# Recurrent mixer's projections: order of the mixtures, key norms by head, and the tail before the scan

## The chip, the cores and the metric

One core of a Trainium2 chip runs the whole program. The metric is the device time of one execution in microseconds; the time of a kernel is the median of its runs. One further execution was taken with the profiler on, and all durations of single instructions are from that one.

## The reference

The program computes two transformer blocks one after the other on 256 tokens of 1024 features. The change touches one part of the second block, the projections in front of an RWKV-7 scan, over 256 context tokens and 256 latent tokens (512 columns):

```python
def rwkv_project(h, shifted, mu, w_rkv, w0, w1, w2, a0, a1, a2, g1, g2, kvec):
    xx = shifted - h
    xr, xw, xk, xv, xa, xg = (h + xx * mu[i] for i in range(6))
    r = xr @ w_rkv[0]
    k = xk @ w_rkv[1]
    v = xv @ w_rkv[2]
    lw = jnp.einsum("zblr,zrd->zbld", jnp.tanh(jnp.einsum("bld,zdr->zblr", xw, w1)), w2) + w0[:, None, None, :]
    decay = jnp.exp(-jnp.exp(-jax.nn.softplus(-lw.astype(jnp.float32)) - 0.5))
    a = jax.nn.sigmoid(a0 + (xa @ a1) @ a2)
    g = jax.nn.sigmoid(xg @ g1) @ g2
    kk = to_heads(k * kvec[0], RW_HEADS).astype(jnp.float32)
    kk = kk / jnp.maximum(jnp.sqrt(jnp.sum(kk * kk, axis=-1, keepdims=True)), 1e-12)
    k = k * (1 + (a - 1) * kvec[1])
```

There are 16 heads of 64 features. The output needs for each head also the bonus, the sum over the head of r k kvec[2], times v, on the latent tokens only; so r and g are computed for 256 columns and k, v, a and the decays for 512.

## The kernel before

The program is written per engine: five instruction streams (TensorE, ScalarE, VectorE, GpSimd and the SyncE queue that issues the loads), each in an order written out by hand, joined by semaphores. `Line` (L63) makes each VectorE, ScalarE and GpSimd instruction wait for the one before it on the same engine. `Tensor.bank` (L159) makes TensorE wait, before it writes one of the eight PSUM banks, for whoever reads the last contents. `mm` is the matrix product (L165 in the profile), `tr` the transpose, here called a turn (L170). VectorE's operations have one line each: `tt` L87 (a product, sum or difference of two tensors), `tsc` L92 or L94, `stt` L98, `copy` L102, `recip` L115. ScalarE's are L138 and L144.

Weights come through a ring of five slots of 128x2048 fp32 (1 MB), in the order that `tile_plan` (L191) lists. SyncE takes the list in turn: it waits until the slot's last tile is used up (`w_free`), then issues the load. `HELD_OUT` (L253) pins the slots of the last tiles, because the scan's scratch lies in slots 0 to 2.

The part around the change is `rwkv_pe` (L2698), `rwkv_act` (L2786) and `rwkv_dve` (L2832). The features lie on the 128 partitions, in 8 tiles, the 512 tokens along the row. One "feature" is one such tile of an output: 8 products of 128x128 weights by 512 columns into one bank (`features`, L2774). The order in which the parts come:

1. VectorE makes the differences XX and then the mixtures h + xx mu, eight `stt` each (`mix`, L2825), in the order of `MIXES` (L2306): w (1), g (5, latent half), a (4), k (2). Two buffers, XMAT[0] and XMAT[1], take them in turn.
2. TensorE does the low-rank products in the order w, g, a (`LOW`, L2307), ScalarE reads them with Tanh, Sigmoid and Copy, and TensorE makes a from the copy (ra2: eight products whose contraction is 64 rows). ScalarE reads each with Sigmoid.
3. TensorE does the eight key features into banks 0 to 3. For each, ScalarE writes KK = key times kvec[0], and VectorE makes K from a and the bank, and the square of KK.
4. The norm block. Eight products with `bones` (ones in two 64x64 blocks) spread each head's sum of squares over its 64 partitions, ScalarE takes eight roots of 128x512, and VectorE does for each tile a maximum, a reciprocal (128x512), and the products into KK and AK. Then VectorE makes the mixtures r (0, latent half) and v (3).
5. TensorE does the eight receptance features (256 columns), then the eight value features (512). Even tiles are copied out by ScalarE, odd ones by VectorE.
6. After the values: VectorE makes r k kvec[2] for 8 tiles, TensorE sums them by head (`bones`), VectorE multiplies with the values; then TensorE turns the values in eight groups of four 128x128 blocks, and VectorE copies each out in four pieces of 64x256.
7. `decay_pe(T, 0)` (L2383): 16 products of 512 columns whose contraction is 64 rows, two into each bank; ScalarE reads each bank with Sigmoid (`decay_act`, L2397). `decay_pe(T, 1)`, the same for the other direction, is issued inside the scan.
8. The scan (`scan_pe`, L2403, and its fellows), two groups of heads against each other through `lead` (L2690), in 17 rounds.

The order of steps 4 and 5 in VectorE's stream is what the change takes apart:

```python
            for k in range(8):
                x = XM[0][:, k, :]
                ve.wait_ge(*n3_ok[k])
                D.tsc(x, x, 1e-12, None, ALU.max, None)
                D.recip(x, x)
                D.tt(KK[:, k, :], KK[:, k, :], x, ALU.mult)
                D.tt(AK[:, k, :], AK[:, k, :], KK[:, k, :], ALU.mult, n4_ok(k))
            mix(D, 4, 256)
            mix(D, 5)
```

In this `mix` the number is a place in `MIXES`, so 4 and 5 are the receptance's and the values' mixtures. `mod_pe` (L933) is not touched; the prediction uses a row of it: a modulation tile is four products of 512 columns over 128 rows into four groups of 32 output rows, set between features of the feed-forward layers.

## Time and profile before

| | |
|---|---|
| median of 3 runs | 3262.8 us (3256.42, 3262.8, 3263.97) |
| the profiled execution | 3254.83 us, its span 3253.0 us |
| TensorE products busy | 2911.7 us, 90% |
| TensorE weight loads busy | 2441.5 us, 75% |
| VectorE busy | 1697.1 us, 52% |
| ScalarE busy | 1215.8 us, 37% |
| GpSimd busy | 117.7 us, 4% |
| mean granted TensorE clock | 0.94 |
| DMA | 349.86 MB, mean 108 GB/s |
| 1 MB weight tile of rkvr, issue to landing | 4.8 us |

The part of the change lies between about 2178 and 2460 us of the span, the scan after it up to about 2955. Busy shares are averages over the whole span. A product of 512 columns in fp32 is recorded as two records, so a feature of 512 columns is 16 records. The end of a product's record is modelled and reaches past the start of the next; the step from start to start is its cost in a full stream. The clock column of a window is the granted share of 2.4 GHz: 1.00 is that level, 0.50 is 1.2 GHz.

### The profile page before, as it was taken

The numbers are of one execution on the slowest core, as the hardware profiler recorded it, in microseconds if no ns is written. First come the engines' busy times: TensorE is split into PE (matmuls) and PEld (weight loads), VectorE is DVE, ScalarE is ACT, GpSimd is POOL, SyncE is SP. The second block draws the span as 40 slices with busy tenths as digits, with TensorE's granted clock in tenths as the row PEclk, the third lists the DMA queues.
The fourth block names the chain that finished last, engine by engine and source line by source line (L and its number), as shares of the span: only waits on it lengthen the run. The fifth ranks groups of instructions, "written<-read, shape, count | busy, mean of one in ns | idle before, by whom it ended". The sixth has DMA issues, their size and how long they took to land.

```text
span 3253.0 us, 65485 instructions
## 1 busy us (share of the span) xinstructions
PE 2911.7 (90%) x28272; PEld 2441.5 (75%) x28272; DVE 1697.1 (52%) x2488; ACT 1215.8 (37%) x1831; POOL 117.7 (4%) x152
## 2 busy tenths in 40 slices
PE   6999999999999989988878998959489999997898
PEld 6977799898778977766657776844337998994886
DVE  4545555454655544215647775443623554555885
ACT  4445554444564443324433323331003334331333
POOL 0000000000000000000000000000001221220000
PEclk9999999999999999989889999979787999998999
DMA  5544344455443543430012432202100000002342
GB/s 208 183 168 170 130 166 178 171 185 187 149 156 137 182 156 133 177 105 2 10 52 91 155 143 108 86 25 102 39 26 9 4 4 16 4 4 95 128 154 104
DMA packets 49983, 349.86 MB, mean 108 GB/s; under 512 B 5792, under 2 KB 5792, under 8 KB 9248
## 3 DMA queue, kind: packets, MB, share of 16 engines
q1 hardware_dynamic: 49248, 343.56, 29.6%
q8 instruction: 225, 3.69, 0.5%
q0 software_dynamic: 448, 2.10, 0.2%
q14 instruction: 62, 0.51, 0.0%
HBM read 344.59 MB, written 1.05 MB: 106 GB/s over the span
## 4 chain that ended last, share of the span: by engine, by line
PE 78%; DVE 13%; ACT 5%; issue 2%; DMA 1%; DVEq 0%; SPq 0%; ACTq 0%
PE psum L165 77%; DVE wide L87 2%; DVE arena L98 2%; DVE arena L87 2%; DVE ring_low L87 2%; ACT w_high L144 1%; DVE wide L115 1%; DMA ring<-in_evt 1%; DVE wide L102 1%; ACT wide L138 1%; ACT arena L140 1%; DVE wide L98 1%; PE psum L170 1%; DMA ring<-in_f_gu 1%; ACT wide L144 0%
## 5 line engine op out<-in xcount | busy, mean ns | idle before, releaser
L87 DVE TENSOR_TENSOR ring_low<-ring,w_high 128x2048 fp32r<-128x2048 f32 (+3 forms) x254 | 560.3, 2206 | 595.9 <-ACT w_high L144 591.3
L144 ACT ACTIVATE w_high<-ring 128x2048 fp32r<-128x2048 f32 (+3 forms) x254 | 468.9, 1846 | 834.3 <-PE psum L165 485.7
L165 PE MATMUL psum<-x_high,w_high 128*128 128x256 f32 (+1 forms) x2040 | 634.3, 311 | 13.4 <-DVE arena L87 6.7
L165 PE MATMUL psum<-x_high,ring_low 128*128 128x256 f32 (+1 forms) x2040 | 627.1, 307 | 0.0
L165 PE MATMUL psum<-x_low,w_high 128*128 128x256 f32 (+1 forms) x2040 | 627.0, 307 | 0.0
L165 PE MATMUL psum<-wide,ring 64*64 64x64 f32 (+2 forms) x4400 | 414.8, 267 | 77.2 <-DVE wide L98 43.1
L165 PEld LDWEIGHTS psum<-x_high,w_high 128*128 128x128 f32 x2040 | 390.7, 192 | 49.9 <-issue 16.8
L165 PEld LDWEIGHTS psum<-wide,ring 64*64 64x64 f32 (+1 forms) x4400 | 296.0, 146 | 172.1 <-issue 97.1
L165 PEld LDWEIGHTS psum<-x_high,ring_low 128*128 128x128 f32 x2040 | 390.6, 191 | 18.6
L165 PEld LDWEIGHTS psum<-x_low,w_high 128*128 128x128 f32 x2040 | 390.9, 192 | 17.2
L165 PE MATMUL psum<-w_high,x_high 128*128 128x512 f32 (+2 forms) x720 | 281.3, 391 | 15.7 <-issue 13.8
L165 PE MATMUL psum<-ring_low,x_high 128*128 128x512 f32 (+2 forms) x720 | 276.9, 385 | 0.0
L165 PE MATMUL psum<-w_high,x_low 128*128 128x512 f32 (+2 forms) x720 | 276.9, 385 | 0.0
L165 PE MATMUL psum<-wide 64*64 64x64 f32 (+3 forms) x6832 | 242.2, 219 | 9.6 <-ACT wide L144 4.7
L165 PEld LDWEIGHTS psum<-wide 64*64 64x64 f32 (+2 forms) x6832 | 215.0, 133 | 25.5 <-ACT wide L144 8.9
L98 DVE SCALAR_TENSOR_TENSOR arena<-arena,prm 128x256 f32<-128x256 f32 x396 | 192.1, 485 | 14.1
L144 ACT ACTIVATE wide<-psum 128x256 f32<-128x256 f32 (+2 forms) x239 | 108.5, 454 | 225.2 <-PE psum L165 216.6
L165 PEld LDWEIGHTS psum<-w_high,x_high 128*128 128x128 f32 x720 | 139.9, 194 | 52.9 <-issue 23.3
L165 PE MATMUL psum<-w_high,h_high 128*128 128x512 f32 x440 | 172.5, 392 | 4.3 <-DVE ring_low L87 4.3
L165 PE MATMUL psum<-w_high,h_low 128*128 128x512 f32 x440 | 171.9, 391 | 0.0
L165 PE MATMUL psum<-ring_low,h_high 128*128 128x512 f32 x440 | 171.9, 391 | 0.0
L87 DVE TENSOR_TENSOR wide<-wide,psum 128x256 f32<-128x256 f32 (+1 forms) x156 | 86.0, 551 | 159.5 <-PE psum L165 153.7
(191 smaller groups left out, 3498.2 us busy)
## 6 DMA issues: line engine op xcount, KB each, us to landing
ring<-in_f_gu SPq DMA_DIRECT2D x88, 1024.0 KB, 4.8
ring<-in_w_mod SPq DMA_DIRECT2D x48, 1024.0 KB, 5.0
ring<-in_fu SPq DMA_DIRECT2D x44, 1024.0 KB, 4.8
ring<-in_f_dn SPq DMA_DIRECT2D x40, 1024.0 KB, 4.8
ring<-in_w_in SPq DMA_DIRECT2D x28, 1024.0 KB, 4.8
ring<-in_fd SPq DMA_DIRECT2D x20, 1024.0 KB, 4.8
ring<-in_rkvr SPq DMA_DIRECT2D x12, 1024.0 KB, 4.8
ring<-in_w_out SPq DMA_DIRECT2D x8, 1024.0 KB, 4.8
```

Source lines behind the costliest of these rows:

```text
L87: self.done(self.eng.tensor_tensor(o, a, b, op), then)
L98: self.done(self.eng.scalar_tensor_tensor(out=o, in0=a, scalar=s, in1=b, op0=op0, op1=op1), then)
L102: self.done(self.eng.tensor_copy(o, i), then)
L115: self.done(self.eng.reciprocal(o, i), then)
L138: self.done(self.eng.activation(o, i, f, bias=bias, scale=scale), then)
L140: self.done(self.eng.activation(o, i, f, bias=bias, scale=scale, accum_out=total), then)
L144: self.done(self.eng.activation(o, i, ACT.Copy, scale=scale), then)
L165: ins = self.eng.matmul(o, l, r, start=a, stop=z)
L170: ins = self.eng.transpose(o, i, ident[0:i.shape[0], 0:i.shape[0]])
```

## The change

The projections are put in another order and three pieces are done otherwise.

- Mixtures come in the order a, k, w, g, r, v. The products of w and g stand between key features (after the second and the fourth); the tiles rw1 and rg1 move in the load order behind the first and second key tile.
- Key norms: ScalarE squares each key tile out of the bank beside writing KK (six buffers SQUARES). One product per tile with `hs`, 128 rows by 16 columns, adds its heads' sums into one 16x512 block of bank 6, behind the feature two later. One root, one maximum and one reciprocal are taken on 16 rows. Products with a column of the identity, spread over 64 columns, and the 16-row block as moving operand spread each head's value over its 64 partitions, two products per tile, behind receptance features 4 to 7.
- The values' buffer VT moves from XX to another place. After the values, eight rounds on TensorE hold one decay bank, one group of turns and one bonus sum. ScalarE reads the decays and copies one half of the turned values, VectorE the other half and makes the bonus product.
- Two dummy activations on one column (Sqrt, Sigmoid) stand ahead of those uses. The signals are named anew.

The diff, cut (renamed signals, the unchanged halves of moved helpers and assertions of room are left out):

```diff
-    plan.append((("rw1",), dr["rw1"], 1024))
-    plan.append((("rg1",), dr["rg1"], 1024))
     plan.append((("ra1",), dr["ra1"], 512))
     plan.append((("ra2",), dr["ra2"], 1024))
     for i in (1, 0, 2):
-        plan.extend((("rkv", i, j), dr["rkvr"][i, j], WS) for j in range(4))
+        for j in range(4):
+            plan.append((("rkv", i, j), dr["rkvr"][i, j], WS))
+            if i == 1 and j < 2:
+                name = ("rw1", "rg1")[j]
+                plan.append(((name,), dr[name], 1024))
...
-        VT = XX
+        VT = wide[:, 25856:29952].rearrange("p (k t) -> p k t", k=8)
+        SQUARES = [wide[:, 29952 + 512 * i:30464 + 512 * i] for i in range(6)]
+        ROOTS = wide[0:16, 25344:25856]
...
+        MIXES = (4, 2, 1, 5, 0, 3)
+        LOW = {4: ("ra1", 64, 0), 1: ("rw1", 128, 4), 5: ("rg1", 128, 5)}
+        BESIDE_KEYS = {1: 1, 3: 5}
...
+        def head_sums(T, k):
+            if k == 0:
+                T.eng.wait_ge(ld_cxb, 16)
+                T.bank(6, rw_act["root", 0])
+            T.eng.wait_ge(*rw_act["kk", k])
+            T.mm(bank(6)[0:16, :], hs[:, 14 - 2 * k:30 - 2 * k], SQUARES[k % 6], k == 0, k == 7, rw_mm(("kk", k)))
...
         def rwkv_pe(T):
+            low_rank(T, 4)
...
             te.wait_ge(*mix_ok[2])
-            features(T, 1, XM[1], 0, kp_mm, k_ok, None)
-            te.wait_ge(ld_cxb, 16)
             for k in range(8):
-                te.wait_ge(*n1_ok[k])
-                T.bank(4 + k % 4, n3_ok[k])
-                T.mm(bank(4 + k % 4), bones, XM[0][:, k, :], True, True, n2_mm(k))
+                feature(T, 1, k, XM[1], 512, k_ok[k])
+                if k > 1:
+                    head_sums(T, k - 2)
+                if k in BESIDE_KEYS:
+                    low_rank(T, BESIDE_KEYS[k])
+            for k in (6, 7):
+                head_sums(T, k)
             te.wait_ge(*mix_ok[0])
-            features(T, 0, XM[0], 256, rp_mm, r_d, r_a)
+            for k in range(8):
+                feature(T, 0, k, XMH[1], 256, rw_dve["r", k] if k % 2 else rw_act["r", k])
+                if k == 4:
+                    te.wait_ge(*rq_ok[0])
+                for j in (2 * k - 8, 2 * k - 7) if k > 3 else ():
+                    T.bank(4 + j % 4, n4_ok[j])
+                    for a in TWO:
+                        T.mm(bank(4 + j % 4)[64 * a:64 * a + 64, :], ident[0:16, 2 * j + a:2 * j + a + 1].to_broadcast([16, 64]),
+                             ROOTS, True, True, rw_mm(("kb", j)) if a else None)
             te.wait_ge(*mix_ok[3])
-            features(T, 2, XM[1], 0, vp_mm, v_d, v_a)
             for k in range(8):
-                te.wait_ge(*bv1_ok[k])
-                T.bank(4 + k % 4, bv_ok[k])
-                T.mm(bank(4 + k % 4)[:, 0:256], bones, BV[:, k, :], True, True, bv_mm(k))
...
-            te.wait_ge(*vz_ok[3, 1])
-            decay_pe(T, 0)
+                feature(T, 2, k, XM[1], 512, rw_dve["v", k] if k % 2 else rw_act["v", k])
+            te.wait_ge(*rw_act["v", 6])
+            te.wait_ge(*rw_dve["v", 7])
+            for i, (tb, g) in enumerate(ITEMS):
+                decay_item_pe(T, 0, tb, g, 4 + i % 4)
+                T.bank(i % 2, rw_dve["vz", i], vz_a[i])
+                trs(T, [(bank(i % 2)[:, 128 * a:128 * a + 128], VT[:, 4 * g + a, 128 * tb:128 * tb + 128]) for a in FOUR],
+                    rw_mm(("vz", i)))
+                T.bank(2 + i % 2, rw_dve["bv", i])
+                te.wait_ge(*rw_dve["rk", i])
+                T.mm(bank(2 + i % 2)[:, 0:256], bones, BV[:, i, :], True, True, rw_mm(("bv", i)))
+            te.wait_ge(*rw_dve["bv", 7])
+            te.wait_ge(*vz_a[7])
             lead(scan_pe(T, 0), scan_pe(T, 1))
...
         def rwkv_act(A):
             for k in range(8):
                 se.wait_ge(*tile_done(1, k))
-                A.act(KK[:, k, :], bank(k % 4), ACT.Identity, kk_ok(k), scale=kv[:, 0, k:k + 1])
-            for k in range(8):
-                se.wait_ge(*n2_mm[k])
-                A.act(XM[0][:, k, :], bank(4 + k % 4), ACT.Sqrt, n3_ok(k))
+                A.act(KK[:, k, :], bank(k % 4), ACT.Identity, scale=kv[:, 0, k:k + 1])
+                if k > 5:
+                    se.wait_ge(*rw_mm["kk", k - 6])
+                A.act(SQUARES[k % 6], bank(k % 4), ACT.Square, rw_act(("kk", k)), scale=kv[:, 0, k:k + 1])
+                if k in BESIDE_KEYS:
+                    low_act(A, BESIDE_KEYS[k])
+            A.act(small[:, 216:217], ident[:, 0:1], ACT.Sqrt)
+            se.wait_ge(*rw_mm["kk", 7])
+            A.act(ROOTS, bank(6)[0:16, :], ACT.Sqrt, rw_act(("root", 0)))
...
+            A.act(small[:, 216:217], ident[:, 0:1], ACT.Sigmoid)
+            for i, (tb, g) in enumerate(ITEMS):
+                decay_item_act(A, 0, tb, g, 4 + i % 4)
+                se.wait_ge(*rw_mm["vz", i])
+                value_rows(A, i, 0, vz_a(i))
...
         def rwkv_dve(D):
+            mix(D, 4, XM[0])
+            mix(D, 2, XM[1])
+            ve.wait_ge(*w_free[("ra1",)])
+            mix(D, 1, XM[0])
             for k in range(8):
...
-                if k == 0:
-                    ve.wait_ge(*w_free[("ra1",)])
-                D.tt(XM[0][:, k, :], KK[:, k, :], KK[:, k, :], ALU.mult, n1_ok(k))
+                if k == 1:
+                    ve.wait_ge(*w_free[("rw1",)])
+                    mix(D, 5, XMH[0], 256)
+                if k == 3:
+                    mix(D, 0, XMH[1], 256)
+            ve.wait_ge(*rw_act["root", 0])
+            D.tsc(ROOTS, ROOTS, 1e-12, None, ALU.max, None)
+            D.recip(ROOTS, ROOTS, rq_ok(0))
+            ve.wait_ge(*w_free["rkv", 1, 3])
+            mix(D, 3, XM[1])
+            for k in (1, 3):
+                receptance_block(D, k)
+            for j in (0, 1):
+                unit_keys(D, j)
+            receptance_block(D, 5)
+            for j in (2, 3, 4, 5):
+                unit_keys(D, j)
+            receptance_block(D, 7)
+            for j in (6, 7):
+                unit_keys(D, j)
...
+            for i in range(8):
+                ve.wait_ge(*rw_mm["vz", i])
+                value_rows(D, i, 1, rw_dve(("vz", i)))
+                if i == 0:
+                    ve.wait_ge(*rw_act["v", 6])
+                ve.wait_ge(*rw_mm["bv", i])
+                D.tt(BV[:, i, :], bank(2 + i % 2)[:, 0:256], VT[:, i, 256:512], ALU.mult, rw_dve(("bv", i)))
```

`unit_keys` waits for its spread root and does the two products into KK and AK; `receptance_block` waits for a receptance feature and copies it out; `value_rows` copies two 64x256 pieces of the turned values. In the new `mix` the number is the mixture's own.

## Rows read from the trace of the kernel before

**Rows 1.** The page's part 4: the chain that ended last, by engine.

```profile
PE 78%; DVE 13%; ACT 5%; issue 2%; DMA 1%; DVEq 0%; SPq 0%; ACTq 0%
```

**Rows 2.** Windows: stretch, length, busy time of each engine (instructions), granted clock, DMA.

```profile
2183.79:2216.48 32.69, 29.01 (x64) 12.46 (x64) 16.02 (x25) 7.66 (x11) 0.00 (x0) 0.86 0.28 97
2216.48:2271.72 55.24, 55.24 (x130) 24.62 (x130) 13.47 (x21) 5.50 (x8) 0.00 (x0) 1.00 0.22 76
2271.72:2321.64 49.92, 6.83 (x16) 2.66 (x14) 47.13 (x44) 6.75 (x10) 0.00 (x0) 0.60 0.06 21
2321.64:2351.75 30.11, 30.11 (x129) 26.16 (x130) 7.27 (x11) 1.53 (x4) 0.00 (x0) 0.93 0.31 105
2351.75:2406.69 54.94, 54.90 (x128) 23.94 (x126) 2.50 (x5) 3.67 (x5) 0.00 (x0) 1.00 0.05 20
2406.69:2431.10 24.41, 9.80 (x49) 6.46 (x49) 21.49 (x49) 0.00 (x0) 0.00 (x0) 0.81 0.13 43
2431.10:2459.45 28.35, 27.66 (x32) 10.36 (x32) 0.00 (x0) 4.78 (x8) 0.00 (x0) 0.50 0.00 0
2459.45:2472.50 13.05, 8.60 (x126) 7.67 (x128) 3.23 (x6) 3.63 (x6) 1.77 (x2) 0.50 0.12 41
...
2209.45:2216.48 7.03, 7.03 (x16) 2.88 (x16) 0.00 (x0) 4.81 (x7) 0.00 (x0) 1.00 0.44 151
```

**Rows 3.** Groups of instructions by form, VectorE, 2160 to 2460: busy us, mean ns, idle before.

```profile
L115 DVE RECIPROCAL wide<-wide 128x512 f32<-128x512 f32 x8 | 26.8, 3353 | 0.3
L98 DVE SCALAR_TENSOR_TENSOR wide<-wide,prm 128x512 f32<-128x512 f32 x32 | 24.1, 752 | 7.0 <-PE psum L165 5.9
L87 DVE TENSOR_TENSOR wide<-wide 128x512 f32<-128x512 f32 x24 | 16.6, 692 | 0.9
L102 DVE COPY wide<-psum 64x256 f32<-64x256 f32 x32 | 13.5, 422 | 1.6
...
L87 DVE TENSOR_TENSOR wide<-psum,wide 128x256 f32<-128x256 f32 x8 | 3.4, 425 | 0.9
```

**Rows 4.** Timeline, ScalarE: start, length, form, idle before and releaser.

```profile
2193.80 0.60 ACT L138 ACTIVATE wide<-psum 128x512 f32<-128x512 f32 x1 [23.27 <-PE psum L165]
```

**Rows 5.** The chain in order of time: start, length, what.

```profile
2208.72 0.73 issue
```

**Rows 6.** Timeline, TensorE, around one modulation tile.

```profile
1752.69 0.39 PE L165 MATMUL psum<-x_low,w_high 128*128 128x512 f32 x1
1752.92 0.39 PE L165 MATMUL psum<-x_high,ring_low 128*128 128x512 f32 x1
1753.23 1.07 PE L165 MATMUL psum<-ring,arena 128*32 128x512 f32 x8
1754.23 0.50 PE L165 MATMUL psum<-x_high,w_high 128*128 128x512 f32 x1
1754.57 0.39 PE L165 MATMUL psum<-x_low,w_high 128*128 128x512 f32 x1
```

**Rows 7.** Groups by form, ScalarE, 2160 to 2460.

```profile
L138 ACT ACTIVATE wide<-psum,prm 128x512 f32<-128x512 f32 x16 | 11.0, 687 | 52.1 <-PE psum L165 52.1
...
L138 ACT ACT_TABLE_LOAD x5 | 6.4, 1283 | 0.4
```

**Rows 8.** Timeline, TensorE, turns of the values.

```profile
2414.41 1.91 PE L170 MATMUL psum<-cst,wide 128*128 128x128 f32 x16
```

**Rows 9.** Windows again: second decays; after the values; around a modulation tile.

```profile
2685.50:2699.50 14.00, 14.00 (x36) 5.90 (x32) 0.42 (x1) 4.89 (x8) 0.00 (x0) 1.00 0.00 0
...
2420.00:2431.00 11.00, 2.60 (x12) 1.56 (x10) 9.87 (x24) 0.00 (x0) 0.00 (x0) 0.58 0.00 0
1740.00:1780.00 40.00, 40.00 (x190) 30.46 (x189) 28.08 (x48) 11.85 (x14) 0.00 (x0) 1.00 0.40 144
```

**Rows 10.** Timeline, TensorE, groups of 32 records in the scan.

```profile
2466.62 1.97 PE L165 MATMUL psum<-wide 64*64 64x64 f32 x32 [0.79 <-DVE wide L87]
...
2681.44 1.10 PE L165 MATMUL psum<-wide 64*64 64x64 f32 x32
```

More of the change, by code:

```diff
@@ L2695, in tile_done, with low_rank, feature @@
         def tile_done(i, k):
-            return w_free["rkv", i, k // 2] if k % 2 else {1: kp_mm, 0: rp_mm, 2: vp_mm}[i][k // 2]
+            return w_free["rkv", i, k // 2] if k % 2 else rw_mm["rkv"[i], k]
+        def low_rank(T, i):
+            name, rows, b = LOW[i]
+            te = T.eng
+            te.wait_ge(*landed((name,)))
+            te.wait_ge(*mix_ok[i])
+            w = raw((name,))
+            x, cols = (XMH[0], 256) if i == 5 else (XM[0], 512)
+            T.bank(b, rw_act["low", i])
+            for k in range(8):
+                T.mm(bank(b)[0:rows, 0:cols], w[:, rows * k:rows * k + rows], x[:, k, :], k == 0, k == 7,
+                     w_free((name,)) if k == 7 else None)
+        def feature(T, i, k, x, cols, taken):
+            key = ("rkv", i, k // 2)
+            T.eng.wait_ge(*landed(key))
+            w = raw(key)
+            T.bank(k % 4, taken)
+            for c in range(8):
+                o = 256 * c + 128 * (k % 2)
+                T.mm(bank(k % 4)[:, 0:cols], w[:, o:o + 128], x[:, c, :], c == 0, c == 7,
+                     None if c < 7 else w_free(key) if k % 2 else rw_mm(("rkv"[i], k)))
+        def head_sums(T, k):
[4 more added lines that the diff above has]
+            T.mm(bank(6)[0:16, :], hs[:, 14 - 2 * k:30 - 2 * k], SQUARES[k % 6], k == 0, k == 7, rw_mm(("kk", k)))
         def rwkv_pe(T):
@@ L2887, in rwkv_dve @@
[L2887 to L2897 removed]
+                D.copy(VT[:, k, :], bank(k % 4), rw_dve(("v", k)))
```

168 lines of the change are left out of this document (70 added, 98 removed).

## The prediction

> **What bounds the kernel now.** I read the chain that ended last first: 78% of the span is TensorE, 13% VectorE [rows 1]. As an average that says nothing of the edited stage, so I cut that stage out by windows of the span [rows 2]. TensorE is full (busy time equal to the window) in four of the eight stretches: key features 55.24, receptance 30.11, values 54.94, decays about 28. It is not full in the other four: 32.69 us from the first mixture to the first key feature, 49.92 us between the last key feature and the first receptance feature, 24.41 us after the values, and the step into the scan. In the 49.92 and the 24.41 VectorE is busy 47.13 and 21.49 us: it is the bound there. Of its rows in the region [rows 3], 8 reciprocals of 128x512 take 26.8 us, 3.35 each. The decay stretch is full but runs at clock 0.50, the 1.2 GHz level, after a stretch in which TensorE was mostly waiting.
>
> **The change part by part.** Durations are those of the profiled execution (3254.83 us, span 3253.0), 8 us under the 3262.8 median, inside the spread of the three runs (7.5 us) but for half a microsecond. The change's sum is made on it and taken off the median.
>
> *A, mixtures by need.* Before, keys start 32.69 us after the first mixture. Now VectorE makes mixture 4 first (about 6.3 us as before, 0.2 later for the small okv operation) and TensorE runs ra1 at once: 8 products of 512 columns out of a cold start. The first low-rank group before took 10.0 us from 2183.79 to its reader at 2193.80 [rows 4]. Then the copy of TA, 0.73 us of TensorE's time [rows 5], then the eight ra2 products, 7.03 us (2209.45 to 2216.48, the last of [rows 2]). Keys start after 0.2 + 10.0 + 0.73 + 7.03 = 18.0 us. Mixture 2 (6.3 us) is long made, mixture 1 ends about 16.5 us in. **-14.7 us.** The DMA queue: the two moved loads stand behind k0 and k1 in it, the first five slots still fill in the feed-forward tail, rg1 waits only for ra1's slot and k2 for ra2's; both are free 20 us or more before use, and a load of 1 MB lands in about 5 us (4.8, table ahead). I cost the queue at nothing. If a slot came late the keys would wait for that one load, 5 us.
>
> *B, the key stage gets longer.* rw1 and rg1 move in: 8 products at 55.24/64 = 0.86 us, and 8 at half the columns, 6.9 + 3.4 = 10.3 us. Eight head sums move in: 0.86 each for 512 columns, however few the output rows. They change the array's shape in the middle of full features. A row that shows such a change is the modulation tile [rows 6]: four products in four column groups, eight records, start at 1753.23; the feature before started at 1752.92 and the second after at 1754.57, and of these 1.65 us two steps of 0.23 (1752.69 to 1752.92) were due anyway, so tile and changes took 1.19 us against 0.86 for one product: up to 0.34 for in and out. The step into and out of ra2 shows 0.17 (7.03 against 8 x 0.86). I take 0.25. The Trainium skill, "TensorEngine Tiling (Array Packing)", section "Key Properties", says that changing the tiling mode drains TensorE, and it speaks against this change; the trace agrees, at these prices. The round trips number 8 here, 4 in the receptance stage and 8 in the tail: 5.0 us in all, ends 0 and 6.8. Stage B: 10.3 + 8 x 1.11 = **+19.2 us**. ScalarE has two 512-wide passes per feature, 0.69 us each [rows 7], and up to three table loads of 1.28; its turn is 6.9 us, so nothing waits. VectorE's mixtures 5 and 0 (half the columns, so under the 6.3 us of a whole one) fit between two key tiles likewise. The last head sum needs the square of tile 7, 1.4 us after the last feature, and two sums stand before it: no wait.
>
> *C, the norm block.* The 49.92 us goes: receptance features need only mixture 0, made beside the keys. What becomes of its VectorE work: 8 squares (0.69, as every 512-wide product [rows 3]) move to ScalarE; 8 reciprocals become one on 16 rows, same 512 columns, so about 3.4 us; 16 products of 128x512 stay (11 us), and mixture 3 (6.3 us) with them. They now stand beside receptance, 35 us long. The chain root, maximum, reciprocal ends 5 us into it and mixture 3 at 11; TensorE asks for the first spread root at 17. Eight pairs of products at 1.4 us follow pairs of spreads, each behind a 3.4 us feature. What would be late next is the value stage's first bank, and it is not. **-49.9 us.**
>
> *D, receptance.* Eight features of half width from a warm start: 8 x 3.43 = 27.5. Eight spread roots come in, each of two products of 512 columns on the same 16 rows into two column halves. No row has 16 rows by 64 columns. Ends: side by side 0.86 for the two, one after the other 1.72. The nearest row is the modulation tile, four products over the same 128 rows in four column groups in little more than one product's time [rows 6], so I take 0.86: 8 x 0.86 + 4 x 0.25 = 7.9. 35.4 against 30.1: **+5.3 us**, serial +12.2.
>
> *E, values.* 54.94 us stay.
>
> *F, the tail.* Before: 52.8 us from the last feature to the scan, 24.41 and 28.35. Bonus sums, 32 turn copies of 0.42 and eight bonus products stood on VectorE in a row with TensorE waiting, then 16 decay products at 1.2 GHz. Now eight rounds of two decay products, four turns and one bonus sum. Warm, 1.72 + 0.48 (four turns; 16 took 1.91 [rows 8]) + 0.43 + 0.25 = 2.9 us. ScalarE has three passes of at most 0.69 in a round [rows 7], VectorE two copies of 0.42 and a product of 0.43: both under 2.9, so TensorE sets the pace. 0.75 for the last value's copy, 8 x 2.88 = 23.0, and 0.9 for the last copies and product: 24.7. **-28.1 us.** The eight products r k kvec (under 0.75 each, the whole-width row of their kind [rows 3]) move under the values, covered by 55 us.
>
> Warm is the assumption. A decay's product on 64 rows ran at 1.2 GHz before, all 28 us, and did not rise. But the same 16 products for the other direction, issued inside the scan with the clock up, ran 14.0 us at 1.00 [rows 9]. And the stage before this tail is the value stage, at 1.00. So I take warm; cold costs 8 x 2.63 = 21 us more.
>
> *G, start of the scan.* The first scan round ran at the low level to 2472.5 [rows 2]: 32 records took 1.97 us there, 1.10 later [rows 10]. About five such groups stood on the chain, so up to 4 us come back if the clock is still up. The round waits much, and the clock fell in the waiting stretch 2420 to 2431 [rows 9]. Ends 0 and 4; I take 3. **-3 us.**
>
> Sum: -14.7 + 19.2 - 49.9 + 5.3 - 28.1 - 3.0 = **-71.2 us**, a span near 3182, and 3262.8 - 71.2 = 3191.6.
>
> **The rivals.**
>
> *1. Spread roots one after another.* The two halves share their rows. For it: no row has this shape. Against it: [rows 6]. It costs 8 x 0.86 = 6.9 us: 3198.5. The Trainium skill, "TensorE: Matmul & The Clock Gate", section "Part 3: Packing small matmuls — row/col tiling", says a weight load overlaps running products only when its row group differs, which would make this the case; the modulation tile, same rows and four column groups, speaks against the rule. Chance 0.13.
>
> *2. The tail runs at 1.2 GHz.* The decays before did so while full. The 0.75 us wait, or the 64-row products with turns between, would let the clock fall. Cost 21 us, and the 3 of G: 71.2 - 24 = 47.2, 3215.6. Against it: ra2's 64-row products and the second decays stayed at 1.00 [rows 2, 9]. Chance 0.10.
>
> *3. Slower.* The clock falls in the key stage, where 16-column sums cut the features, and stays down. Then every feature costs double: keys with what moved in +74, receptance +35, values +55, in all 164 us, of which the 71 gained are only a part: about 3355. It decides from the point where 81 us of warm work (the 71 and 10 more) run at the low level, that is all of the keys and a quarter of receptance. For it: the 28 full microseconds at 0.50. Against it: the window 1740 to 1780 with a modulation tile between features is at 1.00 [rows 9], and the key features ran at 1.00 right after 64-row products [rows 2]. Chance 0.03: 0.02 for that much or more, 0.01 for a fall that eats between 61 and 81 us and leaves the time within 0.3%.
>
> *4. The 49.9 us is not freed,* because receptance waits for something in the norm chain after all: a spread root's bank, or mixture 3 ahead of VectorE's copies of banks 1 and 3. The order written out leaves VectorE some 4 us at the tightest place: its copy of bank 3 ends 14.2 us into the stage, the first spread root 18.2. If half came back as waits, 46 us would be left, 3217; if all, 21, 3241. Chance 0.04.
>
> **How the numbers follow.** The forecast's case has 0.70. The low end of the range is that case with no cost for shape changes (5 us) and the whole 4 us of G, 3185.6, and the 6.4 us by which the fastest run lies under the median: 3179. The high end takes in rivals 1 and 2: 3216. Left out are rivals 3 and 4 and the far sides. This kernel's measurement tells a difference from about 0.3%, 10 us. Faster by more than that: 0.96 (the forecast's case, rivals 1 and 2, and 0.03 of rival 4); within: 0.02 (0.01 of rival 3, and 0.01 of rival 4 for waits beyond those I can name); slower: 0.02.
>
> **What would show it.** Right: no gap of over 3 us between the last key feature and the first receptance feature; one reciprocal of 16x512 near 3.4 us in place of eight; first key feature near 2202; scan's first product near 2391; decay records at 1.02 us length, clock 1.00 from 2194 on. Spread roots: starts of two pairs 0.9 us apart, or 1.7 for rival 1. Wrong: decay records at the low level (rival 2); clock under 1.00 in the features (rival 3); TensorE's idle time in receptance ended by VectorE's products or reciprocal (rival 4).

## The result and the profile after

| | before | after |
|---|---|---|
| median of 4 runs each | 3262.32 us (3256.42 to 3263.97) | 3188.69 us (3182.56 to 3193.04) |
| the profiled execution | 3254.83 us, span 3253.0 | 3182.56 us, span 3180.4 |
| TensorE's first low-rank product to the scan's first product | 275.66 us | 206.58 us |

The ratio is 0.9776, with a 95% interval of 0.9753 to 0.9799: 73.6 us faster by the medians, where the forecast said 71.2 and a time of 3191.6. In the profiled executions the span fell by 72.6 us, and the edited stage (last line of the table, 2183.79 to 2459.45 before, 2184.92 to 2391.50 after) by 69.1.

The page of the changed kernel, its first part and the chain by engine:

```profile
PE 2900.4 (91%) x28304; PEld 2432.8 (76%) x28304; DVE 1658.3 (52%) x2450; ACT 1222.3 (38%) x1849; POOL 117.8 (4%) x152
...
PE 78%; DVE 13%; ACT 5%; issue 2%; DMA 1%; DVEq 0%; SPq 0%; ACTq 0%
```

As before [rows 1], the averages say nothing of the change. Windows of the changed kernel, cut where its stage changes from one kind of work to the next (columns as in [rows 2]):

```profile
2184.92:2201.10 16.18, 15.45 (x32) 5.36 (x32) 11.96 (x16) 6.68 (x9) 0.00 (x0) 0.91 0.11 32
2201.10:2275.04 73.94, 73.94 (x178) 30.95 (x177) 17.43 (x32) 13.75 (x20) 0.00 (x0) 1.00 0.27 91
2275.04:2310.90 35.86, 35.86 (x161) 25.86 (x160) 20.66 (x29) 2.52 (x7) 0.00 (x0) 1.00 0.31 106
2310.90:2366.10 55.20, 55.20 (x130) 24.24 (x128) 8.01 (x14) 3.87 (x6) 0.00 (x0) 1.00 0.06 19
2366.10:2391.50 25.40, 23.50 (x81) 10.86 (x80) 10.92 (x25) 11.30 (x25) 0.00 (x0) 1.00 0.17 53
2391.50:2404.00 12.50, 7.53 (x130) 6.57 (x132) 3.65 (x7) 3.12 (x6) 1.77 (x2) 0.68 0.06 22
2404.00:2415.44 11.44, 10.63 (x240) 10.22 (x241) 4.61 (x8) 3.43 (x8) 3.07 (x4) 0.76 0.01 3
```

They are: a's low rank and a itself; keys with what moved in; receptance with the spread roots; values; the tail; and the scan's first round in two pieces. From 2201.10 to 2366.10 TensorE is full at 1.00: the 49.92 us stretch of [rows 2] has no successor, because receptance starts on the heels of the last head sum. What is left of VectorE's work in it stands beside receptance, where VectorE is busy 20.66 of 35.86 us. VectorE by form, 2165 to 2400 of the changed kernel, the lines that answer to [rows 3]:

```profile
L87 DVE TENSOR_TENSOR wide<-wide,psum 128x512 f32<-128x512 f32 x16 | 11.0, 688 | 8.5 <-PE psum L165 7.8
...
L102 DVE COPY wide<-psum 64x256 f32<-64x256 f32 x16 | 6.8, 427 | 13.5 <-PE psum L170 13.2
...
L115 DVE RECIPROCAL wide<-wide 16x512 f32<-16x512 f32 x1 | 3.3, 3340 | 0.0
```

One reciprocal of 3340 ns stands where eight of 3353 stood. With the same 512 columns, 16 rows took what 128 rows took. TensorE's timeline of the changed kernel (start, length, form, records, idle before and releaser):

```profile
2184.92 8.43 PE L165 MATMUL psum<-wide,ring 128*64 128x512 f32 x16 [16.07 <-issue]
2194.08 34.77 PE L165 MATMUL psum<-wide,ring 64*128 64x512 f32 x80 [0.73 <-issue]
...
2228.78 1.03 PE L165 MATMUL psum<-wide,cx 128*16 128x512 f32 x2
2229.74 7.13 PE L165 MATMUL psum<-wide,ring 128*128 128x512 f32 x16
2236.80 1.03 PE L165 MATMUL psum<-wide,cx 128*16 128x512 f32 x2
...
2272.36 2.75 PE L165 MATMUL psum<-wide,cx 128*16 128x512 f32 x6
2275.04 17.53 PE L165 MATMUL psum<-wide,ring 128*128 128x256 f32 x80
2292.50 1.93 PE L165 MATMUL psum<-wide,cst 16*64 16x512 f32 x8
2294.36 3.72 PE L165 MATMUL psum<-wide,ring 128*128 128x256 f32 x16
...
2366.93 1.09 PE L165 MATMUL psum<-ring,wide 64*128 64x512 f32 x2 [0.83 <-issue]
2367.87 1.02 PE L165 MATMUL psum<-ring,cst 64*128 64x512 f32 x2
2368.82 0.66 PE L170 MATMUL psum<-cst,wide 128*128 128x128 f32 x4
2369.31 0.60 PE L165 MATMUL psum<-wide,cx 128*128 128x256 f32 x2
2369.84 1.12 PE L165 MATMUL psum<-ring,wide 64*128 64x512 f32 x2
...
2391.50 1.09 PE L165 MATMUL psum<-cx,wide 64*64 64x128 f32 x16 [1.08 <-DVE wide L87]
2395.03 0.68 PE L165 MATMUL psum<-wide,ring 64*64 64x64 f32 x16 [2.43 <-DVE wide L87]
...
2397.07 1.97 PE L165 MATMUL psum<-wide 64*64 64x64 f32 x32 [0.79 <-DVE wide L87]
```

Steps from start to start are the prices. A head sum among features: 2228.78 to 2229.74, 0.96 us. The feature behind it steps 7.06 us (2229.74 to 2236.80), where a feature between features stepped 6.90 (55.24/8). So sum and feature together take 8.02 us against 6.90 + 0.86: a round trip of the array's shape costs about 0.26 us here, part of it in the feature. A block of spread roots, two tiles by two halves in eight records: 2292.50 to 2294.36, 1.86 us, so 0.93 for each pair. A tail round: 2366.93 to 2369.84, 2.91, and 2.93 for those that follow.

### The profile page after: what moved, and what is told of

It reads as the page before. It is cut to its first block, busy times and chain, and to the rows that moved or that the text cites. A ratio compares the mean times of both kernels' runs of the same rounds, so it can differ in the third digit from the quotient of the medians.

```text
span 3180.4 us, 65560 instructions
## 1 busy us (share of the span) xinstructions
PE 2900.4 (91%) x28304; PEld 2432.8 (76%) x28304; DVE 1658.3 (52%) x2450; ACT 1222.3 (38%) x1849; POOL 117.8 (4%) x152
## 4 chain that ended last, share of the span: by engine, by line
PE 78%; DVE 13%; ACT 5%; issue 2%; DMA 1%; DVEq 0%; SPq 0%; ACTq 0%
PE psum L165 77%; DVE arena L98 3%; DVE wide L87 2%; DVE ring_low L87 2%; DVE arena L87 2%; ACT w_high L144 1%; PE psum L170 1%; DMA ring<-in_evt 1%; ACT arena L140 1%; ACT wide L138 1%; DMA ring<-in_f_gu 1%; DVE x_low L87 0%; ACT L138 0%; DVE wide L98 0%; DVE ntmp L94 0%
## 5 line engine op out<-in xcount | busy, mean ns | idle before, releaser
L165 PE MATMUL psum<-wide,ring 64*64 64x64 f32 (+3 forms) x4400 | 410.9, 266 | 30.3 <-issue 16.8
L165 PEld LDWEIGHTS psum<-wide,ring 64*64 64x64 f32 (+2 forms) x4400 | 292.6, 145 | 126.9 <-issue 97.1
L144 ACT ACTIVATE wide<-psum 128x256 f32<-128x256 f32 (+3 forms) x255 | 114.5, 449 | 242.7 <-PE psum L165 233.1
L87 DVE TENSOR_TENSOR wide<-wide,psum 128x512 f32<-128x512 f32 (+1 forms) x164 | 91.4, 558 | 168.8 <-PE psum L165 162.6
```

The source lines that it names most:

```text
L87: self.done(self.eng.tensor_tensor(o, a, b, op), then)
L144: self.done(self.eng.activation(o, i, ACT.Copy, scale=scale), then)
L165: ins = self.eng.matmul(o, l, r, start=a, stop=z)
```

## The experiments

All are edits of the changed kernel. The stage's length within one execution is the sharper measure: the changed kernel, profiled again on another chip, gave 206.58 us again. One part of it varies with the same code: the first low-rank group took 8.4 us in some executions and 9.8 in others. It took 9.8 in "norm work first", "both", "spread roots at full width", "spare products" and "four edits together"; 1.4 us of the excess of these five is not the edit's. What lies outside it moves more. In the profiled executions the stage began between 2184.9 and 2200.1 us with the same code ahead of it, and what lies behind it, where only the spare products touch the code, took 785.8 to 794.2 us. "Total" is the difference of medians to the kernel before, measured on the same chip. Where the changed kernel was measured in the same series, excess by medians and excess by stage agree within 3.3 us (20.2 and 18.4, 42.7 and 39.4). In the other series of several runs that bear on the stage alone, the totals lie 2.5 to 6.0 us further from -72.3 than the stage says, so I read no cause from them.

| kernel | stage, us | over 206.58 | ratio, 95% interval | total, us |
|---|---|---|---|---|
| changed kernel again | 206.58 | 0 | 0.9779 (0.9765 to 0.9794) | -72.3 |
| wide reciprocal | 213.76 | +7.2 | 0.9816 (0.9801 to 0.983) | -59.5 |
| norm work first | 220.73 | +14.2 | 0.9828 (0.9812 to 0.9845) | -55.6 |
| both | 233.93 | +27.4 | 0.9872 (0.9858 to 0.9887) | -39.6 |
| both, r's mixture behind | 245.94 | +39.4 | 0.9912 (0.9897 to 0.9926) | -29.6 |
| norm first, r's mixture behind | 224.95 | +18.4 | 0.9845 (0.9829 to 0.9861) | -52.2 |
| spread roots at full width | 220.08 | +13.5 | one run: 3199.0 us | -59.4 |
| old order of mixtures | 212.61 | +6.0 | 0.9809 (0.9786 to 0.9831) | -63.0 |
| old tail | 230.09 | +23.5 | 0.9869 (0.9854 to 0.9883) | -42.8 |
| old tail, decays first | 215.53 | +9.0 | 0.9818 (0.9802 to 0.9835) | -59.4 |
| spare products | 207.97 | +1.4 | 0.9781 (0.9764 to 0.9798) | -71.6 |
| four edits together | 205.50 | -1.1 | 0.9767 (0.9753 to 0.9782) | -76.4 |

The expectation for the changed kernel's second run, which came out in all three points (0.9779, 206.58 us, the group of 32 records at 1.97 us again):

> The changed kernel itself once more, for comparison within this call: 0.976 to 0.980 of the kernel before; stage 206.6 us within 2 us (the phase of the clock at its cold start), the clock low in the first scan round again.

### Are the 49.9 us won by fewer rows or by another place?

**Wide reciprocal**, in the new place:

```diff
-            D.tt(KK[:, j, :], KK[:, j, :], bank(4 + j % 4), ALU.mult)
+            D.recip(SQUARES[j % 6], bank(4 + j % 4))
+            D.tt(KK[:, j, :], KK[:, j, :], SQUARES[j % 6], ALU.mult)
...
-            D.tsc(ROOTS, ROOTS, 1e-12, None, ALU.max, None)
-            D.recip(ROOTS, ROOTS, rq_ok(0))
+            D.tsc(ROOTS, ROOTS, 1e-12, None, ALU.max, None, rq_ok(0))
```

> The changed kernel, but the maximum alone is taken on 16 rows and the reciprocal is taken again on 128x512, once per key tile, after the spread (8 x 3.35 us on VectorE in place of one). Theory (the gain comes from where the norm work stands, beside receptance and values): receptance grows from 35.9 us by the wait for spread-root banks at its end, some 3 us, and values not at all; total +3 to +5 us over the changed kernel, still about 66 to 70 us under the kernel before. Rival (the gain comes from narrowing the reciprocal to 16 rows): the 26.8 us of reciprocals come back on the path, +23 us or more.

Timeline, TensorE, of this kernel, the end of receptance:

```profile
2315.70 1.07 PE L165 MATMUL psum<-wide,cst 16*64 16x512 f32 x4
2320.41 1.79 PE L165 MATMUL psum<-wide,cst 16*64 16x512 f32 x4 [3.64 <-DVE wide L87]
2322.13 3.78 PE L165 MATMUL psum<-wide,ring 128*128 128x512 f32 x4
```

The last pair of spread roots waits 3.64 us for VectorE's product on the tile four before it, and restarts at the low level (1.79 us for a pair whose records take 1.07 before it; the granted clock is 0.56 from 2320.41 to 2322.13). The values behind it start low too (0.66 up to 2330) and take 57.83 us, not 55.20. So the 23.5 us of extra reciprocals cost 7.2, about half of it wait (3.64) and half of it clock. I had expected 3 to 5, all of it wait: the clock's part was missing.

**Norm work first**: `unit_keys` for all eight tiles ahead of receptance on both engines, mixture 3 behind it; narrow reciprocal.

```diff
             for k in (6, 7):
                 head_sums(T, k)
+            te.wait_ge(*rq_ok[0])
+            for j in range(8):
+                T.bank(4 + j % 4, n4_ok[j])
...
             te.wait_ge(*mix_ok[0])
...
+            for j in range(8):
+                unit_keys(D, j)
             ve.wait_ge(*w_free["rkv", 1, 3])
             mix(D, 3, XM[1])
```

> The changed kernel, but the whole norm work (16-row root and reciprocal, eight spread roots, sixteen products) stands before the first receptance feature, as before the change, and the values' mixture behind it. Theory (place and narrowing each suffice for most of the gain): TensorE idles about 5 us for the root and reciprocal, then the spreads go at VectorE's pace, 8 x 1.4 us, of which 8 are the spreads' own that leave receptance: about +8 us over the changed kernel. Rival (place alone made the gain): +25 us or more.

**Both** edits:

> Both undone: norm work before receptance, and eight reciprocals of 128x512. Theory (the two overlap, either alone hides most of the 50 us): stretch between last key feature and first receptance feature about 43 us (root 3, eight tiles of 3.35 + 1.4 with gaps, 5.0 each), so +34 to +38 us over the changed kernel, far more than the sum of the two single undoings (3 to 5, and 8). Rival (effects add up): +11 to +13 us.

The two timelines of TensorE, norm work first and then both:

```profile
2276.77 2.75 PE L165 MATMUL psum<-wide,cx 128*16 128x512 f32 x6
2284.41 13.91 PE L165 MATMUL psum<-wide,cst 16*64 16x512 f32 x32 [4.90 <-DVE wide L115]
2298.26 22.11 PE L165 MATMUL psum<-wide,ring 128*128 128x256 f32 x91
```

```profile
2299.77 1.97 PE L165 MATMUL psum<-wide,cst 16*64 16x512 f32 x4 [2.94 <-DVE wide L87]
2301.67 20.45 PE L165 MATMUL psum<-wide,ring 128*128 128x256 f32 x80
2326.41 8.80 PE L165 MATMUL psum<-wide,ring 128*128 128x256 f32 x28 [4.29 <-DVE hc L102]
```

Both expectations missed. The first gave 14.2 us for 8, of which 1.4 is the longer first low-rank group. The wait for root, maximum and reciprocal was in the expectation and came as said, 4.90 us for 5. What it had wrong is the clock behind that wait. It took the spreads at VectorE's pace, 8 x 1.4 = 11.2 us. A window shows them at the low level, with TensorE busy throughout:

```profile
2284.41:2298.26 13.85, 13.85 (x32) 3.53 (x33) 9.65 (x14) 0.00 (x0) 0.00 (x0) 0.50 0.00 0
```

That is 8 x 1.73 us, twice a product's 0.86, and receptance behind it starts at 0.50 too: receptance and values take 85.0 us together, where 27.5 + 55.2 would do with the clock up. The second gave 27.4 us (26.0 without the longer first group) for 34 to 38, and lies above its rival's 11 to 13 as well; the stretch from the last head sum to receptance was 24.2 us and not 43. There TensorE waits for VectorE only as long as the four banks are taken: when the last spread root is written, four tiles of VectorE's work are still to do, and receptance runs over them until its copies are late (4.29 us). What would have made it wait for all eight tiles is the old place of r's mixture, behind them. That was the next question.

**Both, and r's mixture behind the norm work**, and the same with the **narrow** reciprocal:

```diff
-                if k == 3:
-                    mix(D, 0, XMH[1], 256)
...
             for j in range(8):
                 unit_keys(D, j)
+            mix(D, 0, XMH[1], 256)
```

> Norm work before receptance with eight reciprocals of 128x512, and now the receptance mixture too behind it, as in the kernel before (the run before this had it beside the keys). Theory (what was missing there: TensorE waited only for the banks of four tiles, and with the mixture behind all eight it must wait for all of VectorE's chain): last head sum to first receptance feature 44 to 46 us, stage 38 to 41 us longer than in the changed kernel's 206.6. Rival (the mixture's place is worth nothing): +27 us, as in that run.

> The same old order with the reciprocal on 16 rows. Theory: 4.9 us for root and reciprocal, some 14 for eight tiles, 4.2 for the mixture, 2.5 for a cold start: stage 17 to 20 us longer than the changed kernel's; so in the old order narrowing alone is worth 20 to 23 us, where beside receptance it was worth 7. Rival (narrowing is worth the same anywhere): 31 to 34 us longer.

Timelines of TensorE, receptance's start in the wide kernel and in the narrow one:

```profile
2325.16 5.21 PE L165 MATMUL psum<-wide,ring 128*128 128x256 f32 x16 [21.85 <-DVE wide L98]
```

```profile
2281.39 13.92 PE L165 MATMUL psum<-wide,cst 16*64 16x512 f32 x32 [4.90 <-DVE wide L115]
2300.99 4.46 PE L165 MATMUL psum<-wide,ring 128*128 128x256 f32 x10 [5.68 <-DVE wide L98]
```

Both came as expected, 39.4 for 38 to 41 (the stretch to receptance was 46.1 us, for 44 to 46) and 18.4 for 17 to 20. The wait for the mixture is 21.85 us in the one and 5.68 in the other. So the number of rows is worth 245.94 - 224.95 = 21.0 us in the old order, close to the 7 x 3.35 = 23.5 of reciprocals saved, and 7.2 in the new place: it matters less where TensorE has other work. Of the 39.4 us, the new place alone (r's mixture included) gives 39.4 - 7.2 = 32.2, the 16 rows alone 39.4 - 18.4 = 21.0. The two gains don't add.

### Do the column halves of the spread roots run side by side?

**Spread roots at full width**: each of the two products has 128 columns of weights and writes the whole bank, so the two stand on the same columns. This kernel scales each tile by its second head's norm alone.

```diff
-                        T.mm(bank(4 + j % 4)[64 * a:64 * a + 64, :], ident[0:16, 2 * j + a:2 * j + a + 1].to_broadcast([16, 64]),
+                        T.mm(bank(4 + j % 4), ident[0:16, 2 * j + a:2 * j + a + 1].to_broadcast([16, 128]),
```

> The changed kernel, but each spread root is made by two products of 16 rows by 128 columns into the whole bank, one over the other, in place of two of 64 columns into its two halves. So each tile is scaled by its second head's norm, part of the computation is changed. Two products over the same columns can't run side by side. Theory (the halves ran side by side, 0.86 us for two): receptance +8 x 0.86 = +6.9 us, 35.9 to 42.7. Rival (the halves already ran one after another, as the same row group would have it): receptance unchanged within 1 us.

Its timeline of TensorE, and two of its windows:

```profile
2297.14 4.80 PE L165 MATMUL psum<-wide,cst 16*128 16x512 f32 x8
2301.87 5.95 PE L165 MATMUL psum<-wide,ring 128*128 128x256 f32 x16
2307.75 3.69 PE L165 MATMUL psum<-wide,cst 16*128 16x512 f32 x8
2311.38 3.72 PE L165 MATMUL psum<-wide,ring 128*128 128x256 f32 x16
```

```profile
2297.14:2301.87 4.73, 4.73 (x9) 1.55 (x8) 1.38 (x2) 0.38 (x1) 0.00 (x0) 0.76 0.18 73
2301.87:2307.75 5.88, 5.88 (x17) 4.56 (x16) 1.38 (x2) 0.00 (x0) 0.00 (x0) 0.61 0.00 0
```

A block with as many records takes 3.63 us at full width (2307.75 to 2311.38) and 1.86 in halves: the halves did run side by side, and rival 1 falls. The receptance stage took 46.25 us, 10.4 more than in the changed kernel and not 6.9. Four blocks at 3.63 for 1.86 are 7.1 of it; the other 3.3 are clock, and 1.7 us more of it fell into the values (56.87 us); with 9.8 us for the first low-rank group this makes up the stage's 13.5. In the first block and the feature after it the granted clock was 0.76 and 0.61 although TensorE was busy all the time; the feature took 5.88 us instead of 3.65. Below, under what was not expected, I come back to it.

### What is the interleaved tail worth, and is it clock or overlap?

**Old tail**: bonus sums, then turns, with all copies on VectorE, then the decays. **Old tail, decays first**: the same pieces, with `decay_pe(T, 0)` right behind the values. The diff is the first kernel's; in the second its last line stands ahead of the bonus sums.

```diff
-            for i, (tb, g) in enumerate(ITEMS):
-                decay_item_pe(T, 0, tb, g, 4 + i % 4)
...
+            for k in range(8):
+                te.wait_ge(*rw_dve["rk", k])
+                T.bank(4 + k % 4, rw_dve["bv", k])
+                T.mm(bank(4 + k % 4)[:, 0:256], bones, BV[:, k, :], True, True, rw_mm(("bv", k)))
...
+            te.wait_ge(*rw_dve["vz", 7])
+            decay_pe(T, 0)
```

> The changed kernel with the tail as before: after the values all bonus sums and products, then all turns with VectorE alone copying them out in four pieces, then the sixteen decay products. Theory: the stretch from the last value feature to the scan goes back from 25.4 us to about 49 (the eight r k kvec products stay under the values), half of it decays at 1.2 GHz for 27.7 us: +23 to +25 us. Rival (the tail's gain was only the cold clock): +14 us, with the decays at 1.00 all the same being impossible in that case.

> As the sequential tail, but the sixteen decay products come first, right behind the value features, then bonus sums and turns one after the other on VectorE. Theory (a 64-row product keeps the clock that it finds: warm if it follows full features): decays in 13.8 us at clock 1.00, then 21 us of bonus and turns at VectorE's pace: tail 35 us, +10 us over the changed kernel, and 14 us under the sequential tail, which is the clock's part. Rival (64-row products alone run at 1.2 GHz once they have the engine for themselves): decays 21 to 27 us with clock under 0.8, total +17 to +23 us.

Windows: the wait for VectorE's copies and the decays in the old tail; the decays ahead of it all:

```profile
2386.24:2393.82 7.58, 1.11 (x4) 0.71 (x4) 6.76 (x16) 0.00 (x0) 0.00 (x0) 0.50 0.00 0
2393.82:2422.18 28.36, 27.67 (x32) 10.52 (x33) 0.00 (x0) 4.78 (x8) 0.00 (x0) 0.50 0.00 1
```

```profile
2372.31:2386.24 13.93, 13.93 (x34) 5.91 (x33) 0.69 (x1) 4.18 (x7) 0.00 (x0) 1.00 0.21 75
```

The same 16 products take 28.36 us (27.67 busy) when they follow a wait, and 13.93 when they follow the values. Both expectations held: 23.5 for 23 to 25, and 9.0 for about 10. Of the old tail's 23.5 us, 230.09 - 215.53 = 14.6 are the clock and 9.0 the work done side by side. This old tail is 49.1 us long, where the kernel before had 52.76: its eight products r k kvec stay under the values.

### What is the order of the mixtures worth?

**Old order of mixtures**: w, g, a, k, with all three low-rank groups ahead of the keys and rw1, rg1 back at the front of the loads.

```diff
-        MIXES = (4, 2, 1, 5, 0, 3)
+        MIXES = (1, 5, 4, 2, 0, 3)
-        BESIDE_KEYS = {1: 1, 3: 5}
+        BESIDE_KEYS = {}
```

> The changed kernel with mixtures and low-rank products in the old order w, g, a, k before the keys, and the weights loaded in the old order. Theory: first mixture to first key feature goes from 16.2 us back to 32.7, and 10.3 us of low-rank products leave the key stage: +6 us net. Rival (the later key start is hidden, or the first stretch's gain is not net): 0 to +1 us; or +16 us if the low-rank products in the key stage cost nothing.

As expected: 6.0 us of stage. Its stage began later than any other (2200.07), which belongs to the variation ahead of the stage and not to the edit.

The three sets of edits, each undone by itself, cost 39.4 (norm block: place, rows, r's mixture), 23.5 (tail) and 6.0 (mixtures), 68.9 in all, against the 69.1 us by which the stage fell. That it agrees so closely is partly luck, because two of them undo something other than the kernel before. The norm block undone keeps the head sums as products of 16 columns: from the first key feature to the last value feature it takes 204.4 us, 194.1 without the 10.3 of w and g, against 190.2 before, so its 39.4 is 3.9 too much. The tail undone is 3.7 too short, as said. The place of the gain is shown; what each part is worth is good to about 4 us.

### The start of the scan

Before, the scan took 23.11 us from its first product to a certain later one of its first rounds (2459.45 to 2482.56); after, the same work took 23.94 (2391.50 to 2415.44), though the tail ahead of it ran at 1.00. **Spare products**, whose results nobody reads, fill TensorE's waits there, two ahead of the scan and 17 in its first round:

```diff
+            T.bank(7)
+            for _ in TWO:
+                T.mm(bank(7)[:, 0:256], ident, cst[:, 0:256], True, True)
             te.wait_ge(*rw_dve["bv", 7])
...
+                    fill(10)
...
+                    fill(3)
...
+                    fill(2)
...
+                    fill(2)
```

> The changed kernel, with spare products of 128x128 by 128 or 256 columns put into TensorE's waits at the start of the scan (two of 256 columns before it, 17 of 128 in the first round, into a bank not yet used; results are not read). Theory (the clock fell there because TensorE stood waiting, 1.1 us before and 2.4 us inside the first round): the clock stays at 1.00 through the first round and the stretch from the scan's first product to the one at 23.9 us later shrinks by 4 to 8 us. Rival (the fall comes from the small 64-row products themselves, or from the table of the run): clock falls just the same, and the spare products cost 0 to 3 us.

Windows of this kernel over the same work as the last two of the changed kernel's, and a line of its timeline:

```profile
2401.26:2413.80 12.54, 11.90 (x225) 10.80 (x227) 3.66 (x7) 4.06 (x9) 2.50 (x3) 1.00 0.06 22
2413.80:2420.68 6.88, 5.87 (x183) 5.46 (x180) 4.61 (x8) 2.49 (x6) 2.35 (x3) 1.00 0.01 2
```

```profile
2406.74 1.15 PE L165 MATMUL psum<-wide 64*64 64x64 f32 x32
```

The clock stayed at 1.00, the group of 32 records takes 1.15 us instead of 1.97, and the stretch 19.42 instead of 23.94: 4.5 us, as expected (4 to 8). The 1.4 us by which its stage is longer is the first low-rank group, 9.83 us for 8.43. The last spare product starts at 2409.70. From 2410.30 to 2420.68 TensorE has products of 64 rows alone, is busy 8.85 of 10.38 us, and the clock stays at 1.00; that speaks against the rival that such products bring it down by themselves. The total, -71.6, cannot be told from the changed kernel's.

**Four edits together**: the spare products; head sums in two twos and a four, three round trips of shape in place of six; the decays of two rounds together; and the first decays ahead of the wait for the values' copies.

```diff
+        SUMS_AFTER = {3: (0, 1), 5: (2, 3), 7: (4, 5, 6, 7)}
...
+                if i % 2 == 0:
+                    decay_item_pe(T, 0, tb, 0, 4 + i % 4)
+                    decay_item_pe(T, 0, tb, 1, 5 + i % 4)
```

> The changed kernel with four small things: the spare products at the start of the scan as in the run before; head sums in twos and fours (after key features 3, 5 and 7) in place of one by one, three round trips of shape less; the decay products of two rounds of the tail side by side, four round trips less; and the first decays ahead of the wait for the last value copies. Theory (0.25 us a round trip, 0.8 for that wait, 4.5 for the clock): first low-rank product to the product 23.9 us into the scan goes from 230.5 to about 223.5 us, and the time 7 us under the changed kernel in the same call. Rival (the spare products heat nothing that lasts, the round trips are hidden): 0 to -3 us.

Stage and start of the scan took 205.50 + 19.41 = 224.9 us, against 230.5 and an expected 223.5; 1.4 us of it is again the first low-rank group (9.84). From the first product on a's copy to the first receptance feature it took 80.05 us for 80.96, so 0.3 for each of the three round trips saved. Its median is 4.1 us below that of the changed kernel in the same series (3184.79, 3188.89), where 7 was expected, and the intervals of the two ratios overlap. The 5.6 us within the profiled execution are shown; a gain in the total is likely and not shown.

## Why the prediction was right

Term by term, from the windows:

| term | forecast | measured |
|---|---|---|
| A, keys start | -14.7 | 16.18 - 32.69 = -16.5 |
| B, key stage | +19.2 | 73.94 - 55.24 = +18.7 |
| C, norm block | -49.9 | -49.9 |
| D, receptance | +5.3 | 35.86 - 30.11 = +5.7 |
| E, values | 0 | +0.3 |
| F, tail | -28.1 | 25.40 - 52.76 = -27.4 |
| G, start of the scan | -3 | +0.8 |

**A** was 1.8 us too small. It priced the first low-rank group at the 10.0 us that w's took out of a cold start; here a's group, as many products of as many columns, took 8.43. How soon the clock rises after the first product differs between executions of the same code: it was 0.88 from 2187 to 2190 here, 2.1 us after the first product, and still 0.50 from 2190 to 2193 in "norm work first", as long after its first product, where the group took 9.81. The other 0.2 us is the small operation ahead of the mixture, which lies in front of the first product and so outside the stretch.

**B, D and F** rest on the price of a change of shape, 0.25 us a round trip. The price was right: 0.26 by the rows of a head sum and the feature behind it, and 0.3 by the head sums taken together. What was wrong in B is the number. It counts eight round trips, but the last three head sums stand in a row (2272.36 to 2275.04), so there are six, and 2 x 0.25 is the half microsecond by which 18.7 lies under 19.2. In the tail's round, 2.93 was measured for 2.88. The rule cited from the Trainium skill ("TensorEngine Tiling (Array Packing)", "Key Properties"), that a change of mode drains TensorE, fits these rows; in and out together cost under a third of a full product's 0.86. (The step into and out of ra2 is 7.03 - 6.88 = 0.15, not 0.17; nothing hangs on it.)

**C** held because VectorE's list is so ordered that nothing of the norm work is asked for early. The reciprocal ended at 2279.95 (2276.61 + 3.34), and TensorE came to the first spread root at 2292.50. The wide reciprocal shows where the edge is: with 23.5 us more on VectorE, the last spread root is 3.64 us late.

**Rival 1** is excluded by the blocks of 1.86 and 3.63 us. The rule of the Trainium skill that I set beside it ("TensorE: Matmul & The Clock Gate", "Part 3: Packing small matmuls — row/col tiling"), that weight loads overlap running products only when the row group differs, speaks of loads and not of products; read as I read it, it would have given the changed kernel blocks of at least 3.4 us (4 x 0.86). The trace does not bear out that reading: both halves stand on the same 16 rows, and the block took 1.86 us.

**Rival 2** did not happen, and the old tail shows that such a price is real: there the decays alone cost 14.6 us more at the low level. The 21 us were for the whole interleaved tail, which no run showed at that level. **Rival 3** did not happen in the changed kernel, where every feature ran at 1.00. That its mechanism exists is shown by the full-width spread roots, at about 5 us, since the clock came back by itself. **Rival 4** did not happen; its condition is what the wide and early forms of the norm work bring about.

**G is the step that failed.** It took 3 us for a clock that is up when the scan starts and stays up. It fell: TensorE waits 1.08 us ahead of the scan and 2.43 us after its first group, the clock is 1.00 up to 2395 and 0.50 from 2397 to 2409, and the windows stand at 0.68 and 0.76. The stretch gained nothing. "If the clock is still up" was the condition, and the prediction named the waits of this round; they were in the trace of before (2.44 us after the first group). With spare products in these waits the clock stayed up. That makes the waits the likely cause; a spare product is also one of 128 rows, and which of the two holds the clock was not separated.

Of the 72.6 us of span, 69.1 are in the stage; the stage began 1.1 us later. The other 4.6 lie behind it: 793.55 us before, 788.90 after, the 0.8 of G included. Both kernels have low stretches of the clock there. One, near the end, is in the kernel before and not at the same place in the changed one. Windows of each:

```profile
3190.00:3195.00 5.00, 5.00 (x17) 3.96 (x17) 3.45 (x3) 3.35 (x2) 0.00 (x0) 0.69 0.04 18
```

```profile
3120.00:3125.00 5.00, 5.00 (x24) 4.11 (x23) 4.42 (x2) 3.43 (x3) 0.00 (x0) 1.00 0.16 26
```

"Both, r's mixture behind" has a low stretch there as well (0.66 from 3164 to 3169). The kernels of the experiments, whose code is the same there, took 788.7 to 794.2 us, and 785.8 and 786.9 with the spare products. So these 4.6 us are of the size of what this part varies by, and I don't count them to the change. What sets it was not tried. That the forecast's total came out only 2.4 us off is partly luck: G's miss of 3.8 us and the 5.4 us gained behind it have opposite signs.

## What to carry to other kernels

When an engine waits for another in the middle of a chain, first look for work of its own that does not depend on it and put it there; here, making the other engine's work narrower was worth a third as much once that was done (7.2 us for 21.0). Before pricing a full stretch of small products, look at what stands ahead of it: here, behind a wait of 6.5 us, the stretch took twice as long (28.36 us for 13.93). A credit that holds only if the clock stays up needs the waits of the stretch itself counted.

## What was not expected of the hardware

- **The clock fell under a full TensorE.** In the kernel with full-width spread roots it was 1.00 up to 2299 and 0.50 from 2302 to 2305, with the engine busy throughout (4.73 of 4.73 us in the block of 16 rows by 128 columns, 5.88 of 5.88 in the feature behind it). It fell once more behind the fourth block (0.65 from 2326 to 2329), and not behind the second and third, which were as long. The changed kernel's blocks, also on 16 rows but 1.86 us long, had no fall behind them. The Trainium skill, "TensorE: Matmul & The Clock Gate", "Part 1: The HAM clock gate (the "warmup" mystery)", says that the gate is set by how busy the array has been recently; in these rows the clock was low although the profile shows the engine busy all the time. What sets it off, the rows, the length of the block or where it falls in time, was not separated.
- **The decays, on 64 rows, kept the clock that they found**, in both directions: 27.67 us busy at 0.50 after a wait, 13.93 at 1.00 after the values. So did the spread products of "norm work first", on 16 rows: 13.85 us busy at 0.50 after the wait.
- **With spare products the clock stayed up.** 19 of them, 4.5 us gained in the first scan round.
- **A reciprocal on 16 rows takes 3340 ns, on 128 rows 3353**, both of 512 columns. It was forecast so, but it is seldom seen this plainly: what was saved is the number of instructions.
- **Two column halves on the same rows share the array**: 0.93 us for a pair, 0.91 for one product at full width.
